# FoX and MLA prompt attention with transposed scores in split f32r passes

## The reference

```python
h = rmsnorm(x) * g_attn;  z = h @ w_in                      # 1024 -> 1700 columns
# A: FoX, 4 heads x 64, causal by frame
logits = q @ k.T * 64**-0.5 + cum_q[:, None] - cum_k[None]  # cum = cumsum(log f)
# B: MLA, 8 heads; q = rmsnorm(cq) @ w_uq (64 plain + 32 rotated), k, v = ckv @ w_ukv, one shared
#    rotated key of 32; scale 96**-0.5; causal by chunks of 64
# C: sliding window, 4 q heads / 2 kv heads x 64, own chunk + 2 before, relative bias, sink per head
o = softmax(where(mask, logits, -1e30)) @ v                 # for each of A, B, C
x = x + concat(oA, oB, oC) @ w_out
x = x + square(relu(rmsnorm(x) @ w_up)) @ w_down            # 1024 -> 4096 -> 1024
# after both layers a final rmsnorm; new keys, values, latents and gates are outputs too
```

## Time and profile before

| | |
|---|---|
| time, median of 3 runs | 3073.77 us (3071.0 to 3076.98) |
| profiled execution: its span | 3074.5 us |
| TensorE busy | 2966.2 us, 96% |
| TensorE weight loads busy | 2503.4 us, 81% |
| VectorE busy | 1198.3 us, 39% |
| ScalarE busy | 907.9 us, 30% |
| GpSimd busy | 455.0 us, 15% |
| f32r matmuls of `w_up`, 384 columns (three lines) | 4608 instructions, mean 335 ns |
| f32r matmuls of `w_down`, 512 columns (three lines) | 3456, mean 389 ns |
| transposes of probabilities (L1580) | 984, mean 283 ns |

### The profile page before, as it was taken

One profiled execution on the slowest core, in us unless ns is written; L12 is line 12 of the kernel. 1 busy time (PEld: TensorE's weight loads), 2 busy tenths in 40 slices (PEclk: granted clock), 3 DMA queues, 4 the chain that ended last, 5 costly groups with the idle time before them and its releaser, 6 DMA issues.

```text
span 3074.5 us, 44570 instructions
## 1 busy us (share of the span) xinstructions
PE 2966.2 (96%) x16566; PEld 2503.4 (81%) x16566; DVE 1198.3 (39%) x2555; ACT 907.9 (30%) x1834; POOL 455.0 (15%) x283
## 2 busy tenths in 40 slices
PE   7999999899999999999999999999899999999999
PEld 6975666778999889998979766667788999889987
DVE  3036777524322222222241467775252222222222
ACT  3234544323122112211132344543241222112213
POOL 2110000012222102211111100000121222112223
PEclk9999999899999999999999999999999999999999
DMA  5120001331111101110132100022310111011111
GB/s 194 59 58 15 15 15 41 125 123 35 49 55 48 34 27 55 55 41 21 41 104 62 49 15 15 15 68 98 137 48 22 55 55 41 29 39 55 48 34 68
DMA packets 146935, 166.15 MB, mean 54 GB/s; under 512 B 20032, under 2 KB 117600, under 8 KB 146784
## 3 DMA queue, kind: packets, MB, share of 16 engines
q1 hardware_dynamic: 142464, 157.09, 16.0%
q10 hardware_dynamic: 4320, 7.08, 0.6%
HBM read 134.06 MB, written 30.09 MB: 53 GB/s over the span
## 4 chain that ended last, share of the span: by engine, by line
PE 84%; issue 9%; DVE 2%; ACT 2%; POOL 2%; DMA 1%; SPq 0%; ACTq 0%; DVEq 0%; POOLq 0%
PE ps L1408 21%; PE ps L1409 21%; PE ps L1410 21%; PE ps L1550 7%; PE ps L1580 4%; PE ps L1603 4%; POOL w_lo L698 1%; PE ps L1522 1%; PE ps L1420 1%; ACT pbuf L918 1%; PE ps L1502 0%; PE ps L1505 0%; PE ps L1552 0%; DVE pbuf L1198 0%; PE ps L1454 0%
## 5 line engine op out<-in xcount | busy, mean ns | idle before, releaser
L698 POOL TENSOR_TENSOR w_lo<-w_raw,w_hi 128x1024 fp32r<-128x1024 f32 (+2 forms) x158 | 377.1, 2388 | 2230.6 <-ACT w_hi L773 2230.6
L1408 PE MATMUL ps<-hT_hi,w_hi 128*128 128x384 f32 x1536 | 514.8, 335 | 4.8 <-DVE w_lo L1078 4.8
L1409 PE MATMUL ps<-hT_lo,w_hi 128*128 128x384 f32 x1536 | 514.3, 335 | 0.0
L1410 PE MATMUL ps<-hT_hi,w_lo 128*128 128x384 f32 x1536 | 514.2, 335 | 0.0
L1410 PE MATMUL ps<-w_hi,aT_lo 128*128 128x512 f32 x1152 | 448.4, 389 | 0.0
L1409 PE MATMUL ps<-w_lo,aT_hi 128*128 128x512 f32 x1152 | 448.4, 389 | 0.0
L1408 PE MATMUL ps<-w_hi,aT_hi 128*128 128x512 f32 x1152 | 448.1, 389 | 0.0
L1034 ACT ACTIVATE rbuf<-ps 128x384 f32<-128x384 f32 x192 | 94.5, 492 | 1137.5 <-PE ps L1410 1137.4
L1381 DVE TENSOR_TENSOR x<-ps,x 128x512 f32<-128x512 f32 x288 | 199.2, 692 | 560.2 <-PE ps L1410 560.2
L1373 DVE TENSOR_TENSOR rbuf<-rbuf 128x384 f32<-128x384 f32 x192 | 121.5, 633 | 573.0 <-ACT aT_hi L1036 573.0
L1408 PEld LDWEIGHTS ps<-hT_hi,w_hi 128*128 128x128 f32 x1536 | 289.3, 188 | 5.8 <-DVE w_lo L1078 5.3
(11 more groups left out here) (241 smaller groups left out, 3676.0 us busy)
## 6 DMA issues: line engine op xcount, KB each, us to landing
w_raw<-in_w_up_dram SPq DMA_DIRECT2D x64, 512.0 KB, 4.0
w_raw<-in_w_down_dram SPq DMA_DIRECT2D x64, 512.0 KB, 3.6
residual_scratch<-x SPq DMA_DIRECT2D x18, 512.0 KB, 7.9
x<-residual_scratch SPq DMA_DIRECT2D x18, 512.0 KB, 6.1
w_raw<-in_w_in_dram SPq DMA_DIRECT2D x16, 512.0 KB, 5.2
mixer_scratch<-omixT SPq DMA_DIRECT2D x16, 512.0 KB, 2.6
w_raw<-in_w_out_dram SPq DMA_DIRECT2D x16, 512.0 KB, 6.7
mixin<-mixer_scratch SPq DMA_DIRECT2D x16, 512.0 KB, 8.7
```

Source lines behind the costliest of these rows:

```text
L698: nc.gpsimd.tensor_tensor(w_lo[slot][:, 0:w], raw[i % 2][:, 0:w], w_hi[slot][:, 0:w], ALU.subtract).then_inc(lo_done.sem, 1)
L1408: pe.matmul(out, ah, bh, start=(k == 0), stop=False)
L1409: pe.matmul(out, ah, bl, start=False, stop=False)
L1410: last = pe.matmul(out, al, bh, start=False, stop=(k == n - 1))
```

## The change

`UNITS` now holds the sliding-window units alone, 16 of two heads each, and they run first. FoX and MLA are done afterwards in six pairs of heads (`PAIRS`: fox 0, 1, mla 0 to 3), and a pair goes through 12 steps (`SPANS`): query half 0 (512 queries) against key blocks 0 to 3, query half 1 against key blocks 0 to 7, each step with the queries from the diagonal on.

- `pair_scores` computes transposed scores: a block of 128 keys is stationary, the queries move; three f32r passes of 128 contraction rows (`kh*qh`, `kh*ql`, `kl*qh`). Rows that the head doesn't use are zero; one row holds 1 in `kh` and minus the row maximum in `qh` and `ql` (`MAX_ROW`), so that the maximum is subtracted in the product.
- The exponential on ScalarE writes the probabilities already transposed into a ring of four slots `pt`; there is no transpose and no division before the values. `pair_values` moves up to 512 queries in f32, two heads side by side, two steps behind.
- GpSimd adds the probabilities of the key blocks (`add_probs`, accumulators `acc`), and a product with ones (job `D`) gives the denominator in all partitions; VectorE takes its reciprocal and multiplies the output.
- What the next pair needs is done in jobs between the steps of the current one, over two PSUM banks (`job_bank`): `A`, a pass of untransposed f32r scores (24 chunks of up to 512 keys) whose maximum VectorE takes; `M`, the transpose of the maxima, split into high and low and put by four small DMAs on SP's queue into the rows of `qh` and `ql` (`max_rows`); `K`, `N` (keys and queries from the latents), `R` (rotated queries, with weights prepared by GpSimd, rotated by VectorE with transposed tables), `X` and `F` (high and low parts of them and of FoX), `V` (values). `Q1` and `Q2` make the sample's queries during the last pair.
- SP clears the old maximum rows by DMA (`clear_max_rows`) before the `A` jobs of pairs 2 and later.
- SP stores the output per pair and half (`pair_out`), loads `w_uq` later and the caches at other times; several tiles move. GpSimd clears the unused rows first.
- The layer loop is a Python loop on GpSimd, ScalarE, VectorE and TensorE; on SP it stays.

```diff
+PAIRS = [("fox", 0), ("fox", 1)] + [("mla", m) for m in range(4)]
+SPANS = [(0, b) for b in range(4)] + [(1, b) for b in range(8)]
...
+CHUNKS = [(e, t, c) for t in range(NPT) for e in range(2) for c in range(1 if t < 4 else 2)]
...
+            now += spread([("A", nxt, *ch) for ch in CHUNKS], unit_slots(p, first, NU - 1))
+            now += [((p * NU + NU - 1, 0), ("M", nxt))]
...
+        now += [((p * NU + 3 + LAG_V + 2, 0), ("D", p, 0))]
+        if p > 0:
+            now += [((p * NU + LAG_V, 2), ("D", p - 1, 1))]
...
+                def max_rows(p):
+                    free, count = job_free(("M", p))
+                    sp.wait_ge(free.sem, free.at(l, count))
+                    for e in range(2):
+                        for dst, src in ((qh, mt_h), (ql, mt_l)):
+                            r = MAX_ROW[p % 2][e]
+                            load(dst[p % 2][r:r + 1, e, :].bitcast(F32),
+                                 src[8 * e:8 * e + 8, :].bitcast(F32), m_in)
...
+                for p in range(NP):
+                    if 2 <= p + 1 < NP:
+                        clear_max_rows(p + 1)
+                    pair_out(p, 0)
+                    if p + 1 < NP:
+                        max_rows(p + 1)
...
+                    pair_out(p, 1)
...
+                def add_probs(U):
...
+                    nc.gpsimd.tensor_tensor(A[:, :, off:512], first, T[:, :, 0:n], ALU.add).then_inc(acc_ok.sem, 1)
...
+                    elif kind == "D":
+                        free, _ = job_free(job)
+                        half = job[2]
+                        r = rden[half]
+                        nc.vector.reciprocal(r[:], job_bank(job)).then_inc(free.sem, 1)
+                        free, count = job_free(job)
+                        dve.wait_ge(free.sem, free.at(l, count))
...
+                        nc.vector.tensor_tensor(omix[i][:, halves[half]], bank(4 + half), r[:],
+                                                ALU.mult).then_inc(o2_ok.sem, 1)
...
+                    if kind == "A":
+                        e, t, ch = job[2:]
+                        if (e, t, ch) == CHUNKS[0]:
+                            pe.wait_ge(split_hi.sem, split_hi.at(l, last_of(HI_NO, p)))
+                            if p >= 2:
+                                pe.wait_ge(row_zero.sem, row_zero.at(l, 32 * (p - 1)))
...
+                def pair_scores(p, v, e):
...
+                        pe.wait_ge(m_in.sem, m_in.at(l, 64 * (p + 1)))
+                    if j >= 4:
+                        pe.wait_ge(st_exp.sem, st_exp.at(l, j - 3))
...
+                    pe.matmul(out, kh[i][:, e, keys], qh[i][:, e, qs], start=True, stop=False)
+                    pe.matmul(out, kh[i][:, e, keys], ql[i][:, e, qs], start=False, stop=False)
+                    last = pe.matmul(out, kl[i][:, e, keys], qh[i][:, e, qs], start=False, stop=not diag)
...
+                        last = pe.matmul(bank(4 + half)[half_rows(e), 512 - n:512], vals[:, b, h * HD:(h + 1) * HD],
+                                         pt[U % NPT_RING][:, e, 0:n], start=(b == 0), stop=(b == 4 * half + 3))
```

More of the change, by code:

```diff
@@ L64 @@
 LAG = 4
[L67 to L89, removed]
@@ L119 @@
[L119 to L137, removed]
@@ new lines, with span_cols, spread @@
+NU = len(SPANS)
+LAG_V = 2
+NPT_RING = 4
+def span_cols(v):
+    half, b = SPANS[v]
+    q0 = max(b * P, half * 512)
+    return q0, 512 * (half + 1) - q0
+CHUNKS = [(e, t, c) for t in range(NPT) for e in range(2) for c in range(1 if t < 4 else 2)]
+ROPE_ROW = [[64, 0], [96, 32]]
+MAX_ROW = [[96, 32], [64, 0]]
+def spread(jobs, slots):
+    total = sum(w for _, w in slots)
+    out, done, k = [], 0.0, 0
+    for key, w in slots:
+        done += w
+        while k < len(jobs) and (k + 0.5) / len(jobs) <= done / total + 1e-9:
+            out.append((key, jobs[k]))
+            k += 1
+    assert k == len(jobs)
+    return out
@@ new lines, with last_of @@
+PLAN = plan_jobs()
+JOBS_AT = {}
+JOB_NO, HI_NO, DVE_LO_NO, POOL_LO_NO = {}, {}, {}, {}
+for _key, _job in PLAN:
+    JOBS_AT.setdefault(_key, []).append(_job)
+    if _job[0] not in "FX":
+        JOB_NO[_job] = len(JOB_NO)
+    if _job[0] in ("F", "X", "K", "N"):
+        HI_NO[_job] = len(HI_NO) + 1
+    if _job[0] in ("K", "N"):
+        DVE_LO_NO[_job] = len(DVE_LO_NO) + 1
+    if _job[0] in ("F", "X"):
+        POOL_LO_NO[_job] = len(POOL_LO_NO) + 1
+NJOBS = len(JOB_NO)
+def last_of(table, p):
+    return max([n for job, n in table.items() if job[1] <= p], default=0)
@@ L150, with jobs_on_bank, pool_lows_before, acc_steps @@
+def jobs_on_bank(i, n=NJOBS):
+    return len(range(i, n, 2))
+ACC_STEPS = 11
+ACC_ISSUED = (0, 2, 3, 4, 4, 5, 6, 7, 8, 9, 10, 11)
+def pool_lows_before(U):
+    return sum(1 for key, job in PLAN if job[0] in ("F", "X") and key < (U, 0))
+def acc_steps(U):
+    p, v = divmod(U, NU)
+    return ACC_STEPS * p + (2, 2, 3, 4, 5, 5, 6, 7, 8, 9, 10, 11)[v]
 ITEMS = [("mla", s) for s in range(STREAMS)] + [("swa", p) for p in range(4)] + [("fox", p) for p in range(4)]
@@ L153 @@
 NI = len(ITEMS)
[L154 to L158, removed]
+ACT_CHAIN, POOL_CHAIN = 1, 2 * NT + 7
+DVE_CHAIN = 9 + 3 * NUN + (2 * NI + 6)
 SCALE64 = HD ** -0.5
@@ new lines, in _ @@
+                for half in range(2):
+                    act.wait_ge(kpe_tp.sem, kpe_tp.at(l, half + 1))
+                    for i in range(2):
+                        for e in range(2):
+                            r = ROPE_ROW[i][e]
+                            last = nc.scalar.copy(kh[i][r:r + 32, e, halves[half]], bank(4 + half)[r:r + 32, :])
+                    last.then_inc(kpe_hi.sem, 1)
+                act.wait_ge(kpe_tp.sem, kpe_tp.at(l, 3))
+                nc.scalar.copy(kpeTs[0:ROPE, :], bank(6)[0:ROPE, 0:P]).then_inc(kpe_hi.sem, 1)
@@ L925, in _ @@
+                for U in range(NP * NU + LAG_V):
+                    for pos in range(3):
+                        if U < NP * NU and pos < 2:
+                            pair_exp(U // NU, U % NU, pos)
+                        for job in JOBS_AT.get((U, pos), ()):
+                            job_act(job)
                 act.wait_ge(wk_mm.sem, wk_mm.at(l, 1))
@@ L1064, in _ @@
             dve.wait_ge(cs_in.sem, 16)
[L1066 removed]
+            for l in range(DEPTH):
                 chain = Chain(dve, dve_chain, l)
@@ L1691, in stream_scores @@
                                 else:
-                                    last = add(S[rows, 128:256], q, qkTs[:, 2, new], stop=True)
+                                    last = add(S[rows, 128:256], q, qkTs_s[:, 2, :], stop=True)
                     else:
```

961 lines of the change are left out of this document (638 added, 323 removed).

## The result

The changed kernel takes 3293.7 us (median of 4 runs, 3283.7 to 3307.7) beside 3073.6 us for the kernel before on the same chip: 1.0715 times as long, 95% interval 1.0698 to 1.0733, or 220 us more. I had forecast +151 (3225 us, range 3090 to 3320): the sign and the range held, the size was 69 us short.

A forecast was written before the change was run, and what follows sets the result against it. TensorE, busy 96% of the span, was taken to bound the kernel. Each layer's attention stretch was summed to 416 us against 340.5, +75.5 per layer and +151 for two, giving 3225 us (range 3090 to 3320).

The forecast's parts named there:

- TensorE's work falls, idle time rises: Attention stretch: TensorE's priced work falls about 28 us per layer, but idle time rises from 19 to 90 us or more.
- (1): Stretch before the first window scores: steps wait for stored outputs and both halves of the rotated key; 19 us (14 to 26).
- (2): Sliding-window units running alone: VectorE sets the pace while TensorE has 37 us to do; 58 us (50 to 75).
- (3): Pair ends: next pair's first scores wait for the maximum row's chain and loads; 5.0 us, six times a layer, 30.
- (4): Clearing of the old maximum row, issued behind pair_out: first A products stall 24 us a layer (14 with a short reciprocal).
- (5): First half's denominators amid the A jobs: reciprocal and multiply hold VectorE; 2.2 us, five times, 11 (0 if short).
- (6): Other waits in the pairs: K/N chains 5 us, GpSimd's low parts and additions in fox0 3; GpSimd and ScalarE otherwise covered.
- (7): Stalls at the maximum row and its clearing, ten a layer, lower TensorE's clock; 27 us (0 to 60).
- The work of the pairs: TensorE's products in the six pairs at full-clock prices: 226 us a layer, with 8 us for switches between forms.
- the waits were not covered: Denies the rival that waits are covered and the kernel gets faster: 3053 us, chance 12%.
- the clock did not hold: Denies the rival that the clock holds, without its 27 us a layer: 3171 us, chance 20%.
- the third rival: Clock stays low through most of the pairs, as waits come before it recovers: 60 us more per layer, 3345, chance 13%.

The follow-up runs named there:

- e2: The changed kernel with window scores contracting over all 128 rows in place of 64 (window outputs differ from the reference's); 3266.8 us, ratio 1.0622.
- e7: The changed kernel with window scores over 128 rows, half of the key rows zero, so that the result is right; 3272.8 us, ratio 1.0639.
- e8: On top of e4, four float32 products with unused results fill each wait for the maximum row's loads; 3226.5 us.
- e4: The changed kernel with the clearing of the old maximum row issued ahead of the store of the previous pair's second half; 3252.5 us, ratio 1.0570.
- e6: On top of e4, the maximum row is formed two steps earlier, at the tenth step in place of the twelfth; 3233.0 us.
- e10: The changed kernel with the edits of e4, e6, e7 and e9 together; 3201.8 us, ratio 1.0401.
- e11: The changed kernel with the edits of e4, e7, e8 and e9 together; 3203.2 us.
- e9: The changed kernel with the low parts of the rotated keys moved behind the first two window units; 3280.3 us (runs 3257.5 to 3290.7), ratio 1.0634.
- e3: The changed kernel with one unused full-height float32 product of 512 columns added ahead of each window unit's scores; 3282.8 us, ratio 1.0682.
- e5: The changed kernel with a plain copy in place of the reciprocal of the 512 denominators (pair outputs differ from the reference's); 3241.7 us.

## Why the prediction was right, and where it was mis-sized

- **TensorE's work falls, idle time rises (the argument as a whole): right in direction.** Weighted with the granted clock at each moment, TensorE's busy time in the stretch falls from 316 to 309 us in the first layer and from 316 to 310 in the second: 6 or 7 us, where I had 28. The stretch lost to waits in series and to the clock. In the first layer TensorE is idle 462.1 - 379.4 = 83 us; I had asked for 90 or more beside 19 before. Its busy time did not fall but rose (from 322 to 379), as 0.18 of the stretch's clock was missing: what I had said the row would show was wrong, since I had not put the clock into it.
- **(1) Preparation: mis-sized.** 30.0 us for 19, outside the 14 to 26. I looked at waits for stored outputs. What came last was VectorE's eight subtractions of the rotated keys (0.70 each, at 233.65) and the bias table behind them, 8.2 us in which TensorE waits; 3.2 us more go before the first latent transpose.
- **(2) The window phase: the step that failed.** I had 58 us set by VectorE, over 85% busy, with TensorE near 60%. In the trace VectorE is busy 58.2 of 84.8 us (69%) and TensorE 74.0 (87%): it was TensorE-bound at 0.50, 84.8 us with the first maximum row for my 63, above even the upper end of 75 + 5. I had priced a unit at the full clock and had put the clock loss at 27 us a layer, for the pairs. e2 and e7 show the VectorE-bound phase that I had described, at 70 us, once the products have full height. That is 15 us of clock a layer, and 7 on VectorE's side.
- **(3) The maximum row: right.** Forecast 5.0 us each, in the trace 0.75 + 3.62, and 0.74 + 4.17 for the first.
- **(4) The clearing: right.** Forecast 4, 7, 5.6, 7 (sum 24); trace 2.6, 6.6, 5.4, 6.2 (sum 20.7). The reciprocal: 3.1 us from the slope of the earlier trace rows, 3.36 measured, 4.9 times the copy's 0.69. The Trainium skill, "VectorE: DVE Perf Modes", section "First, the fixed hardware budget", has the divide repeat 8 times, which gave my estimate of 4.3 us. The trace does not agree with that estimate; the line through small rows came nearer.
- **(5) 11 us, trace 8.9; (6) 8 us, trace about 9.** Right.
- **(7) The clock in the pairs: 27 us, trace 32 and 24** (33 for the first with the stages' mean clocks). The mean clock is 0.88 and 0.91 in the two layers. e8 shows the mechanism: filling the waits alone moves it to 0.97.
- **The work of the pairs: 15 us short.** From 651.93 to 653.53 us of the trace six f32r products of 512 columns take 1.60 us, where 6 x 0.227 is 1.36: the first and the last, next to f32 values, take 0.34 and 0.32 and the four between them 0.23 or 0.24. The values behind them take 1.01 where I had 0.93. If all 72 steps of a layer are like this one, that is 72 x 0.32 = 23 us (an estimate) beside the 8 that I gave all form changes. A change between f32r and the bf16 mask costs next to nothing in this trace: after a 512-column product the mask starts 0.24 us later.
- **GpSimd: covered, as said.** Its sums took at most 2.41 us for 1024 elements (forecast 2.4) and it was busy 133 of 347 us in the pairs.
- **The loop written out: 0, right.** From the first MLP product of layer 1 to the layer-2 stretch both kernels take 985 to 988 us. **The sample stage** I had at 0, and it gave 12 us: the same products, at another clock. First layer, before and then after:
```profile
551.74:630.80 79.06, 72.23 (x491) 61.05 (x489) 38.49 (x115) 27.44 (x73) 7.05 (x3) 0.85 0.28 95
```
```profile
673.27:743.83 70.56, 63.54 (x490) 54.21 (x489) 38.69 (x114) 27.12 (x73) 7.07 (x3) 0.98 0.25 82
```
In e4 and e6 this stage fell back to 0.85 and 78 us in the first layer, and in e10 and e11 in the second, though nothing in it differs. So some 8 us of any comparison hang on how the clock happens to stand, and differences between experiments of less than that are not to be read.
- **Small slips in the sums:** 16 units of 2.6 us are 42, not 40.6; the chain of (4) adds up to 8.7, not 8.9; (5) is 3.8 - 2 = 1.8 each, so 9 in place of 11, where the trace has 8.9. None of them bears on the result.
- **The rivals:** the waits were not covered, the clock did not hold, and GpSimd did not bound. A clock that stays low through a whole stage did happen, but in the window phase and not in the pairs, where the third rival had it. Most errors had the same sign; 3293.7 is near the upper end of my likeliest case (3300) and inside the range because that was wide.

What stays open: why the height of these products counts for the clock (the runs show that it does, not how), how much of e6's gain is real beyond 19.5 us, and which part of the runs' spread in e9 is the edit's. Two form changes were seen in few places, and the 23 us above are not tested by a run.

## What to carry to other kernels

Price each stage of TensorE at both clocks, and ask of each what its products look like. Here a stage in which 2.0 of every 5.2 us went to products of 64 rows was busy all the time and stayed at 1.2 GHz, where the same products strewn between others (the kernel before, clock 0.98), or with one taller product more in each unit (e3), did no harm. When work that filled each other's waits is put in sequence, list the waits in series and add the clock: in the changed kernel's pairs it cost 29 us beside 60 idle, about half as much again. Taking out single waits gave back less of it (a quarter to a third in e4 and e5), so the price of the whole is not that of each wait. A load that is issued behind a store in a queue inherits all that the store waits for; where both have been issued by one engine, look at the order before anything else.

## What the runs showed of the hardware

- With TensorE busy without a gap from 270 to 317 us the granted clock stayed at 0.50. The last 64-row scores started at 310.3; the clock was 0.95 in 317 to 319. With the same scores over 128 rows it was 1.00 from 270 to 290 us at 80% busy (e2, real data in all rows) and 0.97 at 84% (e7, half of the key rows zero).
- A reciprocal of 128 x 512 from PSUM took 3357 ns on VectorE, with 3 ns between the fastest and the slowest of 24, beside 692 ns for a copy.
- A VectorE operation with both inputs in SBUF took longer beside GpSimd: the same scaling of 128 x 128 took 1.12 us beside GpSimd's two `lb` products (210.75 to 212.97) and 0.34 behind them.
```profile
211.99 1.12 DVE L1399 SCALAR_TENSOR_TENSOR zc<-zc,lat_rs,gkv_bc 128x128 f32<-128x128 f32 x1
...
213.44 0.34 DVE L1399 SCALAR_TENSOR_TENSOR zc<-zc,lat_rs,gkv_bc 128x128 f32<-128x128 f32 x1
```
